# Bringing the last expert pass to its tokens by products instead of through DRAM

## The reference

```python
gates = sum(one_hot(expert_idx, 16) * weights)      # top-1 group, top-2 experts in it
a, u  = t @ w_gate[e], t @ w_up[e]                  # 1024 -> 256
y     = sum over e of (silu(a) * u * gates[e]) @ w_down[e]
h     = h + y
```

## Time and profile before

| | |
|---|---|
| median of 3 runs | 1306.46 us (1305.32 to 1307.43) |
| the profiled execution, device time | 1307.46 us |
| its span, first to last instruction | 1305.7 us |
| PE busy | 1152.9 us, 88% |
| DVE busy | 467.7 us, 36% |
| ACT busy | 256.2 us, 20% |
| POOL busy | 237.1 us, 18% |
| mean granted TensorE clock | 0.949 of full |
| DMA, mean over the span | 163 GB/s |

### The profile page before, as it was taken

One profiled execution on the slowest core, in us unless ns is written; L12 is line 12 of the kernel. 1 busy time (PEld: TensorE's weight loads), 2 busy tenths in 40 slices (PEclk: granted clock), 3 DMA queues, 4 the chain that ended last, 5 costly groups with the idle time before them and its releaser, 6 DMA issues.

```text
span 1305.7 us, 15254 instructions
## 1 busy us (share of the span) xinstructions
PE 1152.9 (88%) x5795; PEld 717.5 (55%) x5795; DVE 467.7 (36%) x821; ACT 256.2 (20%) x494; POOL 237.1 (18%) x168
## 2 busy tenths in 40 slices
PE   5899999999999999789999865968898879999990
PEld 4889889889788777533333322444444543333330
DVE  6301431431456402612222216264747362122214
ACT  4122132132133111001100003122324200111111
POOL 4233223233244221020000006110000120000004
PEclk8999999999999999889999986979999989999995
DMA  6241132141141114749999933200012285999916
GB/s 263 65 146 64 50 143 67 48 161 49 49 161 33 65 65 183 316 149 299 338 354 345 328 117 131 100 30 1 0 46 83 107 353 162 345 348 355 311 50 225
DMA packets 38673, 212.34 MB, mean 163 GB/s; under 512 B 5376, under 2 KB 5504, under 8 KB 29648
## 3 DMA queue, kind: packets, MB, share of 16 engines
q1 hardware_dynamic: 21168, 151.26, 31.7%
q10 hardware_dynamic: 12704, 43.16, 10.5%
q0 software_dynamic: 4736, 17.04, 3.5%
HBM read 307.78 MB, written 35.78 MB: 263 GB/s over the span
## 4 chain that ended last, share of the span: by engine, by line
PE 62%; DVE 12%; issue 11%; POOL 6%; DMA 6%; ACT 3%; ACTq 0%; POOLq 0%; DVEq 0%
PE ps L772 19%; PE ps L1002 15%; PE ps L1021 8%; POOL ring_r L1967 4%; DMA xT<-slot_rows 4%; PE ps L1096 3%; PE ps L1047 3%; PE ps L990 2%; PE ps L890 2%; PE ps L778 2%; DVE arena L1896 2%; DVE arena L1893 2%; PE ps L979 1%; PE ps L940 1%; ACT arena L1387 1%
## 5 line engine op out<-in xcount | busy, mean ns | idle before, releaser
L1002 PE MATMUL ps<-ring,xT 128*64 128x512 f32 x640 | 226.9, 599 | 5.9 <-DVE xT L1427 5.9
L772 PE MATMUL ps<-x_hi,ring_r 128*128 128x264 f32 x1024 | 191.7, 288 | 2.5 <-DVE xT L1427 2.5
L1967 POOL TENSOR_TENSOR ring_r<-ring,ring_r 128x1024 fp32r<-128x1024 f32 x56 | 134.6, 2418 | 288.9 <-ACT ring_r L1185 288.9
L1002 PE MATMUL ps<-arena,xT 128*64 128x512 f32 x384 | 168.7, 593 | 0.0
L772 PEld LDWEIGHTS ps<-x_hi,ring_r 128*128 128x128 f32 x1024 | 161.2, 191 | 3.1 <-issue 2.9
L1427 DVE TENSOR_TENSOR xT<-ps,gains 128x512 f32<-128x512 f32 (+1 forms) x92 | 57.4, 665 | 262.5 <-PE ps L990 252.9
L772 PE MATMUL ps<-xT_r,ring_r 128*128 128x264 f32 x512 | 146.8, 287 | 0.0
L772 PE MATMUL ps<-ring_r,x_hi 128*128 128x512 f32 x384 | 125.7, 410 | 11.6 <-POOL ring_r L1967 11.6
L1021 PE MATMUL ps<-arena 128*64 128x512 f32 x512 | 122.0, 621 | 6.5 <-ACT arena L1311 6.5
L1002 PEld LDWEIGHTS ps<-ring,xT 128*64 128x64 f32 x640 | 73.1, 139 | 95.2 <-issue 91.9
L772 PEld LDWEIGHTS ps<-xT_r,ring_r 128*128 128x128 f32 x512 | 97.5, 191 | 0.1
(11 more groups left out here) (241 smaller groups left out, 1483.2 us busy)
## 6 DMA issues: line engine op xcount, KB each, us to landing
ring<-in_w_gu SPq DMA_DIRECT2D x46, 2048.0 KB
arena<-in_w_down SPq DMA_DIRECT2D x74, 1024.0 KB
arena<-in_w_gu SPq DMA_DIRECT2D x28, 2048.0 KB
ring<-in_w_ret SPq DMA_DIRECT2D x48, 512.0 KB, 3.5
slot_out<-arena ACTq DMA_DIRECT2D x64, 256.0 KB, 8.8
xT<-slot_rows ACTq DMA_DIRECT2D x60, 256.0 KB, 6.1
slot_rows<-arena ACTq DMA_DIRECT2D x8, 1024.0 KB, 4.2
ring<-in_w_ret_out SPq DMA_DIRECT2D x16, 512.0 KB, 4.5
```

The costliest lines, as they stand in the source:

```text
L772: last = mm(dst, a_parts[x], b_parts[y], start=(start and n == 0), stop=(stop and n == 2))
L1002: last = mm(ps[cols, b, :], xgT[:, k % 2, c, cols], by_row(gu(j))[:, c, :], start=(c == 0), stop=(c == KT - 1))
L1967: G.tensor_tensor(w_lo[slot][:, m], w_raw[slot][:, m], w_hi[to][:, m], ALU.subtract).then_inc(lo_made, 1)
```

## The change

Passes 0 to 14 go through DRAM as before. Pass 15 isn't written to `slot_out`, which is cut to LATE = 1920 rows. Its result stays in `yo`, and each token tile gets its share by a product with a 128 (slots) x tokens matrix of weights.

- After the expert table is made, DVE computes `PL` (slot minus LATE), `WE` (the weights, zero where a token's slot is in pass 15), and `slot_g` (the slot, or 0 where it is in pass 15), which the gathers use as their indices.
- One tile per pass, in passes 2 to 6, DVE makes the tile's matrix (tokens by 128 slots: where iota equals PL, the weight, for both choices, added). A pass later PE transposes it through bank 4 behind down_project, and ACT copies it to `late_w`, which lies where retention's short operands were.
- ACT's `results_of(15)` ends after its copy. Behind down_project(15) PE does `late_results` for all tiles, two products of 512 columns each, on the bank pairs 4, 6, 0, 2, 4. DVE's `add_late` adds a tile's pair of banks to h.
- DVE's order is add_late of the first tile, and then for each tile combine, add_late of the next, and the normalising steps as before. combine waits also for its own tile's add_late.
- POOL starts the gathers when pass 14 has landed. Their destinations are spread over buffers that are free by then; the one of tile 3 is the place of down weights that pass 15 reads, so its gathers wait for pass 15's last product.
- SP's load of the final gain waits for pass 14 instead of 15. The key and value products take banks 6, 7, 4, 5, 6 instead of 4, 5, 6, 7, 4.

```diff
+LATE = SECONDS + (EXPERTS - 2) * BLK
...
-        gat = cv(5, 2, D)
+        gat_at = {META: 10240, 0: 12288, 1: 14336, 2: 27392, 3: 16384}
+        gat = [arena[:, gat_at[t]:gat_at[t] + 2 * D].rearrange("p (n c) -> p n c", n=2) for t in range(5)]
+        late_w = short[:, 0:POS]
...
-        slot_out = nc.dram_tensor("slot_out", (SLOTS, D), F).ap()
+        slot_out = nc.dram_tensor("slot_out", (LATE, D), F).ap()
...
+            fl.phase([(f"OT{l}_{t}", 4) for t in MOE_TILES[l]])
             t_blocks_end[l] = list(fl.total)
+            fl.phase([(f"LC{l}_{t}", (4, 6, 0, 2, 4)[n]) for n, t in enumerate(TILES5[l:])])
...
-        fl.phase([(f"KV{t}", 4 + n % 4) for n, t in enumerate(TILES5)])
+        fl.phase([(f"KV{t}", (6, 7, 4, 5, 6)[n]) for n, t in enumerate(TILES5)])
...
             for j in range(2):
-                sp.wait_ge(mo[1][f"y_out{j}"], in_pair(ROUNDS - 1))
+                sp.wait_ge(mo[1][f"y_out{j}"], in_pair(ROUNDS - 2 - j))
...                                                           # PE
+                def late_weights(n):
+                    t = tiles[n]
+                    name, r = f"OT{l}_{t}", rows(t)
+                    pe.wait_ge(m["late_ready"], n + 1)
+                    fl.wait_free(pe, name)
+                    nc.tensor.transpose(ps[:, 4, 0:r], late_hot[n % 2][0:r], ident[0:r, 0:r]).then_inc(full[4], 1)
...
                     down_project(k - 1)
+                    if k - 3 in range(len(tiles)):
+                        late_weights(k - 3)
...
+            def late_results(l, t):
+                r, at = rows(t), slice(col0(t), col0(t) + rows(t))
+                if t == TILES5[l]:
+                    all_read(pe, t_blocks_end[l])
+                fl.wait_free(pe, f"LC{l}_{t}")
+                b = fl.bank(f"LC{l}_{t}")
+                for c in range(2):
+                    last = mm(ps[0:r, b + c, :], late_w[:, at], yo[:, 1, 512 * c:512 * c + 512], start=True, stop=True)
+                last.then_inc(full[b], 1)
...                                                           # ACT
                     nc.scalar.activation(yo[:, j, 0:512], ps[:, B_YA, :], ACT.Copy).then_inc(free[B_YA], 1)
+                    if k == ROUNDS - 1:
+                        return
...
+                def late_weights(t):
+                    name = f"OT{l}_{t}"
+                    fl.wait_full(act, name)
+                    nc.scalar.activation(late_w[:, col0(t):col0(t) + rows(t)], ps[:, 4, 0:rows(t)], ACT.Copy)\
+                        .then_inc(free[4], 1)
...                                                           # DVE
+                step.done(V_.tensor_scalar(v(PL, 10), v(PLACE, 10), -float(LATE), None, ALU.add))
+                step.done(V_.scalar_tensor_tensor(chosen(WE), chosen(PLACE), float(LATE), chosen(W1), ALU.is_lt, ALU.mult))
+                step(V_.scalar_tensor_tensor(chosen(GF), chosen(PLACE), float(LATE), chosen(PLACE), ALU.is_lt, ALU.mult))
+                V_.tensor_copy(slot_g[:, :, 0:nt], chosen(GF)).then_inc(m["gather_ready"], 1)
+                def late_weights(n):
+                    t = tiles[n]
+                    r, hot = rows(t), late_hot[n % 2]
+                    if n >= 2:
+                        fl.wait_full(dve, f"OT{l}_{tiles[n - 2]}")
+                    for c, dst in enumerate((hot, late_second)):
+                        step.done(V_.tensor_scalar(dst[0:r], iota[0:r], chosen(PL)[0:r, c, t:t + 1],
+                                                   chosen(W1)[0:r, c, t:t + 1], ALU.is_equal, ALU.mult))
+                    step.wait()
+                    V_.tensor_tensor(hot[0:r], hot[0:r], late_second[0:r], ALU.add).then_inc(m["late_ready"], 1)
...
+                def add_late(t):
+                    r, b = rows(t), fl.bank(f"LC{l}_{t}")
+                    fl.wait_full(dve, f"LC{l}_{t}")
+                    V_.tensor_tensor(h[0:r, t, :], flat(ps[0:r, b:b + 2, :]), h[0:r, t, :], ALU.add).then_inc(free[b], 1)
...
+            add_late(TILES5[0])
             for n in range(len(TILES5) + 2):
                 if n < len(TILES5):
                     combine(TILES5[n])
+                if n + 1 < len(TILES5):
+                    add_late(TILES5[n + 1])
...                                                           # POOL
+                pool.wait_ge(m["gather_ready"], 1)
                 for j in range(2):
-                    pool.wait_ge(m[f"y_out{j}"], in_pair(ROUNDS - 1))
+                    pool.wait_ge(m[f"y_out{j}"], in_pair(ROUNDS - 2 - j))
                 for t in TILES5[l:]:
                     r = rows(t)
+                    if t == NT - 1:
+                        round_full(pool, l, B_YB, ROUNDS - 1)
                     for c in range(2):
-                        G.indirect_dma_start(gat[0:r, t, c, :], None, slot_out,
-                                             bass.IndirectOffsetOnAxis(slot_i[0:r, c, t:t + 1], 0))\
+                        G.indirect_dma_start(gat[t][0:r, c, :], None, slot_out,
+                                             bass.IndirectOffsetOnAxis(slot_g[0:r, c, t:t + 1], 0))\
                             .then_inc(m[f"gathered{t}"], 16)
```

More of the change, by code:

```diff
@@ L1049, in key_values @@
                 last.then_inc(full[b], 1)
+            for t in TILES5:
+                late_results(0, t)
             for n in range(len(TILES5) + 1):
@@ L1160, in _ @@
             experts(1)
+            for t in TILES5[1:]:
+                late_results(1, t)
         @block.scalar
@@ L1336, in experts @@
                     results_of(k - 1)
+                    if k - 3 in range(len(MOE_TILES[l])):
+                        late_weights(MOE_TILES[l][k - 3])
                 hidden_of(ROUNDS - 1)
@@ L1788, in experts @@
                     results_of(k - 1)
+                    if k - 2 in range(nt):
+                        late_weights(k - 2)
                 results_of(ROUNDS - 1)
                 def combine(t):
-                    r, n = rows(t), tiles.index(t)
+                    r = rows(t)
                     dve.wait_ge(m[f"gathered{t}"], 32)
-                    step(V_.scalar_tensor_tensor(h[0:r, t, :], gat[0:r, t, 0, :], v(W1, nt)[0:r, t:t + 1],
-                                                 h[0:r, t, :], ALU.mult, ALU.add))
-                    V_.scalar_tensor_tensor(h[0:r, t, :], gat[0:r, t, 1, :], v(W2, nt)[0:r, t:t + 1],
-                                            h[0:r, t, :], ALU.mult, ALU.add).then_inc(m["gath_used"], 1)
-                return combine
-            combine = experts(0)
+                    fl.wait_read(dve, f"LC{l}_{t}")
+                    for c in range(2):
+                        last = V_.scalar_tensor_tensor(h[0:r, t, :], gat[t][0:r, c, :], chosen(WE)[0:r, c, t:t + 1],
+                                                       h[0:r, t, :], ALU.mult, ALU.add)
+                        if c == 0:
+                            step(last)
+                    last.then_inc(m["gath_used"], 1)
+                def add_late(t):
+                    r, b = rows(t), fl.bank(f"LC{l}_{t}")
+                    fl.wait_full(dve, f"LC{l}_{t}")
+                    V_.tensor_tensor(h[0:r, t, :], flat(ps[0:r, b:b + 2, :]), h[0:r, t, :], ALU.add).then_inc(free[b], 1)
+                return add_late, combine
+            add_late, combine = experts(0)
             step = Steps(dve, dsem["attention"])
@@ L1932, in _ @@
                     add_projection(t)
-            combine = experts(1)
+            add_late, combine = experts(1)
             dve.wait_ge(fin_in, 16)
+            add_late(0)
             for n in range(NT + 1):
@@ L1938, in _ @@
                     combine(n)
+                if n + 1 < NT:
+                    add_late(n + 1)
                 if n:
```

17 lines of the change are left out of this document (11 added, 6 removed).

## The result

The changed kernel took 1292.75 us (median of 5 runs, 1290.67 to 1298.04) against 1307.25 us for the kernel before (5 runs). The two medians lie 14.5 us apart. The ratio of the times is 0.9916, 95% interval 0.989 to 0.9941: 11.0 us faster, 7.7 to 14.4. A second measurement gave 0.9928 (0.9905 to 0.9951), 9.4 us. The forecast was 10.9 us less than before, 1295.6 us, with a range of 1292.4 to 1300.2, which holds the 1292.75; its narrower range for the mechanism alone, 1293.5 to 1298, misses it by 0.75 us.

A forecast was written before the change was run, and what follows sets the result against it. TensorE carries most of the span, but the layer ends wait for pass 15's DRAM write and gathers, with VectorE bounding most of the second's tail. 7.3 + 5.2 - 1.6 = 10.9 us less gives 1295.6 us, range 1292.4 to 1300.2.

The forecast's parts named there:

- The sum: Whole kernel: 7.3 us from the first layer's end plus 5.2 from the second's, less 1.6 for transposes, 10.9 us faster.
- First joint: First layer's end, pass 15 to tile 0's transposes: gathers start a pass earlier, then VectorE bounds; 7.3 us earlier.
- The late products: Pass 15's two 128x512 products per token tile on TensorE, costed at 0.43 us each, 0.86 a tile.
- the wait for the meta tile's rstd: First layer's end: rstd, queued behind ten gathers on GpSimd, comes at 785.75 instead of 785.3, so 0.5 us more.
- Second joint: Second layer's tail to the last final norm: gathers 8.0 us earlier, less three adds, plus covered waits; 5.2 us earlier.
- Weight transposes: Nine 128x128 transposes on TensorE inside the passes, 0.24 us each (bounds 0.1 and 0.5), 2.2 in sum, 1.6 taken.
- half should vanish: First layer's passes: DMA is the limit there, so half of that layer's 1.2 us of transposes wouldn't count.
- A: First layer's gathers beside VectorE work grow by 0.64 us each, GpSimd bounds; gain 2.8 instead of 7.3, 1300.1 us; chance 0.12.
- B: First layer: pass 14's write lands late behind the weight load, near 780; gain 0.5 there, 1302.4 us; chance 0.06.
- C: Gathers of late slots all read row 0 and lengthen, costing from 6 us on; 1313.6 us at 24; chance 0.03.
- D: First layer: TensorE's clock back sooner before the key products, 3.0 us saved, 1292.6 us; chance 0.06.

The follow-up runs named there:

- beside: Changed kernel with the nine weight transposes moved from behind the down products to behind the hidden transposes; 1293.05 us, ratio to before 0.9916.
- big_out: Changed kernel with slot_out allocated at its old size of 2048 rows, rows from 1920 on unused; 1295.38 us, ratio to before 0.9921.
- warm: Changed kernel plus seven filler products in the first layer, three ahead of the meta tile's transposes and four behind; 1293.18 us, ratio to before 0.9931.
- weights_only: Kernel before plus only the making of the nine weight matrices; pass 15 still goes through DRAM; 1305.17 us, ratio to before 1.0011.
- gathers_late: Changed kernel, but all gathers wait for the end of pass 15's last down product; 1301.74 us, ratio to before 0.9980.
- fold: Changed kernel, but in the second layer TensorE adds h behind each late product and VectorE's four adds go; 1290.38 us, ratio to before 0.9908.
- gap: Changed kernel plus six filler products before the last pass's hidden transposes in both layers; 1300.85 us, ratio to before 0.9982.
- all: Changed kernel with the edits of beside, warm and fold together; 1289.54 us, ratio to before 0.9910; measured again 1285.22 us, ratio 0.9871.
- nofill: The kernel all without its filler products; 1291.83 us, ratio to before 0.9901.

## Why the prediction was right

**The sum.** The time came out inside the range by the forecast's mechanism, but that 11.0 and 9.4 us stand so near 10.9 is in part luck. The spans of the profiles are 14.8 and 10.2 us apart. In the first pair the terms of the forecast come to 12.1 for the joints, and 3.0 in the first layer's passes, which the forecast didn't have, come on top. In the second pair the joints come to 9.4 instead of 12.5, and 4.2 us more in the second layer's passes (2.0 of it waits for rows, 1.6 the transposes) stand against 3.2 in the first layer's and 2.0 between the layers.

**First joint: 7.3 us forecast, 6.8 and 5.9 measured.** The mechanism is the forecast's to the row: the gathers behind pass 14's landing, then VectorE alone. The first gather stands 2.54 us ahead of the copy, forecast 2.25. Two terms were off. The late products were costed at 0.43 us each; the trace has two instructions of 0.43 for one float32 product, so 1.72 us a tile with both halves, and VectorE's first add starts 2.85 us behind the copy's start and not 1.65. Against that the wait for the meta tile's rstd (0.5 in the sum) didn't come: pass 15's copy was at 772.06, rstd was ready at 783.37, 11.3 us behind it, where 10.9 were forecast, and VectorE reached it later, at 783.72, by what the late products had cost. Net 0.5 us, 16.85 instead of 16.3. The second profile has 16.85 too; its joint is worth 5.9 because the first gather of the kernel before stood 5.27 behind the copy there and not 6.34.

**Second joint: 5.2 forecast, 5.3 and 3.5 measured.** Last norm 22.87 behind the copy, forecast 23.0; first gather 2.69 ahead, forecast 2.7. The second measurement shows what the sum left out: the copy's own time moves by 1.7 us with the clock level of the last down product, and the joint gives most of that back (24.28), since the gathers then come last. The forecast said that it is wrong if either joint shortens by less than 4 us: by that sign the second pair, with 3.5, is a miss of this term. The 23.0 is met where the copy isn't early (22.87 here, 22.6 in `beside` and `big_out`), and missed by 1.2 to 1.3 where it is (24.28, and 24.20 in `warm`).

**Weight transposes: 1.6 net forecast.** Each cost 0.41 us, not 0.24, inside the bounds of 0.1 and 0.5. In the second layer four make 1.6 alone. In the first, five make 2.0 and the waits for rows fall by about as much (7.7 and 7.4 us before, 4.9 and 4.8 after, 5.6 in `weights_only`), which is the "half should vanish" of the forecast and more. The sum came out right because one error covers the other.

**Not forecast: 3.0 us in the first layer's passes.** Before, in both profiles and in `weights_only`, two stretches of 3.4 us at half clock fall into these passes, each 1.7 us of work lost; in the changed kernel (both profiles), `gathers_late`, `beside`, `warm`, `fold`, `gap` and `big_out` it is one; in both profiles of `all` and in that of `nofill` there is none. A window of the kernel before in such a stretch (length, busy us of each engine, clock, DMA share, GB/s):

```profile
750.00:751.00 1.00, 1.00 (x6) 0.36 (x4) 1.00 (x3) 0.00 (x0) 0.00 (x0) 0.50 0.25 102
```

That accounts for 1.7 of the 3.0. Waits for rows are 2.8 us shorter and the transposes cost 2.0, which leaves 0.8; the last 0.5 isn't placed. It isn't DRAM placement (`big_out`), not the weights (`weights_only`) and not the early gathers (`gathers_late`), each by one profile. Why one stretch less falls there is open: each follows a wait of TensorE of 1.8 to 2.9 us, but not each such wait has one behind it, and between otherwise like kernels they stand at different waits (707, 735, 750, 767). That they move with small shifts in time fits, and wasn't tested. So the cause of this term isn't shown.

**The rivals.** A, gathers stretched by VectorE: one gather a layer takes 1.47 and 1.91 us, the others 0.85 to 1.01, and in the changed kernel nothing waits for them; refuted as a bound there. Where the copy is early (`warm`, `fold`, `nofill`), VectorE does wait for the rstd behind the gathers, for 0.6 us. The rule of the Trainium skill (SBUF — State Buffer, Who interferes with whom) that VectorE's two-SBUF-input instructions block only GpSimd's reads fits the issues that ran beside combining steps at 0.94 to 1.01 us, and the long row as little as it did before the change. B, the landing near 780: the first gather at 769.52 refutes it. C, the crowded row 0: in the first layer the data is there when VectorE comes, and in the second tile 0's second gather lands 6.00 us behind its start, where the two profiles of the kernel before have 5.60 and 5.17; the second profile of the changed kernel has 5.71. Gathers lengthen by 0.1 to 0.8 us, not by the 6 from which it would cost; refuted. D, the clock back sooner: the meta tile's products took 8.79 us and its windows show 0.50 from 785 to 794, so it didn't come back by itself; in `warm`, where TensorE is kept busy, it never fell there.

## What to carry to other kernels

When a result that was routed through DRAM is brought by a product instead, look at what the DRAM part then waits for: here the earlier start of the other gathers was worth 4.1 us by the stages and 6.8 by the ratio, as much of the gain as the product that made it possible. When two waits end nearly together, as product and gather do here, moving one alone gives back half of the step or more; move both, or relieve the engine behind them. A gain at one place needs a look at the rest of the run: half clock that falls elsewhere took most of one back here. Count instructions, not products, in the trace before costing one.

## What the runs showed of the hardware that was not expected

- A float32 product of 128x512 is two matmul instructions of 0.43 us each at the upper clock level. A lone 128x128 transpose between a group of products and the next costs 0.41 us, next to other transposes 0.11.
- In the second layer GpSimd's two small steps on 128x1 take 0.19 and 0.55 us while VectorE idles (last tile). Beside VectorE's steps on 128x1024 with both inputs in SBUF they take 1.11 and 1.47 (tiles 1 and 2; 0.19 and 1.42 at tile 0). In the kernels where the VectorE step beside them reads PSUM (`fold`, `all`, `nofill`), they stay at 0.19 and 0.55 to 0.57. GpSimd's timelines of the changed kernel and of `fold`:

```profile
1275.64 1.11 POOL L2035 TENSOR_SCALAR var<-ss 128x1 f32<-128x1 f32 x1 [2.16 <-ACT arena L1205]
1276.84 1.47 POOL L2038 TENSOR_TENSOR rstd<-var,con 128x1 f32<-128x1 f32 x1
```
```profile
1278.17 0.19 POOL L2043 TENSOR_SCALAR var<-ss 128x1 f32<-128x1 f32 x1 [2.55 <-ACT arena L1207]
1278.44 0.55 POOL L2046 TENSOR_TENSOR rstd<-var,con 128x1 f32<-128x1 f32 x1
```

- After a wait of 2.8 us TensorE's next products ran at 1.2 GHz in some kernels and at 2.4 in others (5.35 against 3.65 us for the same sixteen), and seven otherwise useless products kept 24 later instructions at 2.4 GHz, which took 2.3 to 2.7 us off them.
